# Shifting the SBUF addresses of the matmul operands in a fused two-block transformer kernel

## What is computed

```
first_block:  x += g1 * mixer(modulate(rms_norm(x)));  x += g2 * swiglu(modulate(rms_norm(x)), w_ffn_in, w_ffn_out)
              mixer = s5 state space (layer 0), short convolution (layer 1); then rms_norm(x, final_g)
second_block: x = layer_norm(ALPHA*x + mixer(x));      x = layer_norm(ALPHA*x + squared_relu_mlp(x))
              mixer = dilated window attention (layer 0), HGRN2 linear attention (layer 1)
```

## Time and profile before

| | us |
|---|---|
| median of 3 runs | 2748.53 |
| the profiled execution, its own time | 2751.34 |
| its span, first to last instruction | 2749.6 |
| PE busy | 2660.2 (97%) |
| DVE busy | 1490.2 (54%) |
| ACT busy | 1049.2 (38%) |
| POOL busy | 109.3 (4%) |

### The profile page before, as it was taken

How to read it: one execution, slowest core, us unless ns; L and a number is a source line. 1 busy time by engine, 2 the same in 40 slices (tenths; PEclk the granted TensorE clock), 3 DMA queues, 4 the chain that set the end, 5 groups by cost and what they waited for, 6 DMA issues and landing times.

```text
span 2749.6 us, 38093 instructions
## 1 busy us (share of the span) xinstructions
PE 2660.2 (97%) x15914; PEld 2227.6 (81%) x15914; DVE 1490.2 (54%) x2230; ACT 1049.2 (38%) x1496; POOL 109.3 (4%) x118
## 2 busy tenths in 40 slices
PE   5999999999999999999999999999999999999998
PEld 2668888888898888888888887888889888888887
DVE  8958555556463333465555555744336675833335
ACT  3534312223233222255555554522223555522223
POOL 4800000000000000000000000000000000000000
PEclk7999999999999999999999999999999999999998
DMA  5054544432323222322222222132221121233220
GB/s 237 2 202 174 214 184 184 184 123 69 100 93 123 92 92 92 103 75 70 74 77 78 74 70 93 56 106 98 92 106 58 62 97 57 77 107 106 93 93 31
DMA packets 46102, 282.89 MB, mean 103 GB/s; under 512 B 6113, under 2 KB 8545, under 8 KB 19954
## 3 DMA queue, kind: packets, MB, share of 16 engines
q1 hardware_dynamic: 40002, 238.02, 25.1%
q0 software_dynamic: 5936, 42.51, 4.2%
HBM read 278.41 MB, written 2.10 MB: 102 GB/s over the span
## 4 chain that ended last, share of the span: by engine, by line
PE 79%; DVE 14%; ACT 4%; issue 2%; DMA 1%; POOL 0%; DVEq 0%; ACTq 0%
PE PS L646 17%; PE PS L647 17%; PE PS L648 17%; PE PS L781 4%; PE PS L783 4%; PE PS L782 4%; PE PS L870 1%; DVE Wl L1547 1%; PE PS L810 1%; PE PS L811 1%; PE PS L812 1%; DMA adab<-adaw 1%; PE PS L739 1%; PE PS L737 1%; PE PS L738 1%
## 5 line engine op out<-in xcount | busy, mean ns | idle before, releaser
L646 PE MATMUL PS<-Hl,Wh 128*128 128x512 f32 x1256 | 490.5, 391 | 7.2 <-DVE Wl L1547 7.2
L647 PE MATMUL PS<-Hh,Wl 128*128 128x512 f32 x1256 | 489.8, 390 | 0.0
L648 PE MATMUL PS<-Hh,Wh 128*128 128x512 f32 x1256 | 489.8, 390 | 0.0
L1133 ACT CAST Wh<-raw 128x2048 fp32r<-128x2048 f32 (+2 forms) x164 | 294.6, 1842 | 416.3 <-PE PS L648 395.8
L1547 DVE TENSOR_TENSOR Wl<-raw,Wh 128x2048 fp32r<-128x2048 f32 (+2 forms) x164 | 356.0, 2210 | 74.9 <-ACT Wh L1133 74.7
L646 PE MATMUL PS<-Gl,Wh 128*128 128x512 f32 x880 | 347.8, 395 | 0.0
L648 PE MATMUL PS<-Gh,Wh 128*128 128x512 f32 x880 | 347.6, 395 | 0.0
L647 PE MATMUL PS<-Gh,Wl 128*128 128x512 f32 x880 | 347.6, 395 | 0.0
L646 PEld LDWEIGHTS PS<-Hl,Wh 128*128 128x128 f32 x1256 | 236.6, 188 | 57.1 <-DVE Wl L1547 7.9
L648 PEld LDWEIGHTS PS<-Hh,Wh 128*128 128x128 f32 x1256 | 236.5, 188 | 49.6
L647 PEld LDWEIGHTS PS<-Hh,Wl 128*128 128x128 f32 x1256 | 236.5, 188 | 49.1
(11 more groups left out here) (419 smaller groups left out, 4802.5 us busy)
## 6 DMA issues: line engine op xcount, KB each, us to landing
raw<-wstream SPq DMA_DIRECT2D x152, 1024.0 KB, 6.3
raw<-wstream SPq DMA_DIRECT2D x64, 768.0 KB, 4.5
adab<-adaw POOLq DMA_DIRECT2D x40, 1024.0 KB, 5.8
raw<-wstream SPq DMA_DIRECT2D x20, 512.0 KB, 4.0
raw<-adap SPq DMA_DIRECT2D x4, 1024.0 KB, 10.0
ada_land<-adap SPq DMA_DIRECT2D x4, 1024.0 KB, 18.9
X<-xT SPq DMA_DIRECT2D x1, 2048.0 KB, 8.3
XU<-xU SPq DMA_DIRECT2D x1, 2048.0 KB, 14.4
```

The costliest lines, as they stand in the source:

```text
L646: mm(o, Wh[:, s, c0:c0 + P], xl[:, k, :], start=k == 0, stop=False)
L647: mm(o, Wl[:, s, c0:c0 + P], xh[:, k, :], start=False, stop=False)
L648: last = mm(o, Wh[:, s, c0:c0 + P], xh[:, k, :], start=False, stop=k == kt - 1)
L1133: nc.scalar.copy(w_high(p, h, widths[h]), raw[:, h, 0:widths[h]]).then_inc(split_h, 1)
```

## The change

```diff
         X = sb("X", [P, KT, T])
+        cst = sb("cst", [P, 3 * P + 4])
+        ident, ones_d, ones_h = cst[:, 0:P], cst[:, P:2 * P], cst[:, 2 * P:3 * P]
+        NRM = sb("NRM", [P, 5, KT])
+        sq = sb("sq", [P, 2, T])
+        Rn = sb("Rn", [P, T])
         land = ExitStack()
-        ada_land = [sb("ada_land" + str(i), [P, HALF], c=land) for i in range(4)]
+        ada_land = [sb("ada_land" + str(i), [P, HALF], c=land) for i in range(2)]
+        sb("gap_land", [P, 4, KT], c=land)
+        ada_land += [sb("ada_land" + str(i), [P, HALF], c=land) for i in range(2, 4)]
         land.close()
         Gh = sb("Gh", [P, KT, T], F32R)
+        LB = sb("LB", [P, 4, KT])
         Gl = sb("Gl", [P, KT, T], F32R)
         raw = sb("raw", [P, 2, HALF])
-        cst = sb("cst", [P, 3 * P + 4])
-        ident, ones_d, ones_h = cst[:, 0:P], cst[:, P:2 * P], cst[:, 2 * P:3 * P]
-        MODS = sb("MODS", [P, 96])
-        NRM = sb("NRM", [P, 5, KT])
-        AM = sb("AM", [P, 4, KT])
-        LNP = sb("LNP", [P, 8, KT])
-        CW = sb("CW", [P, 3, KT])
-        HG = sb("HG", [P, KT])
-        LB = sb("LB", [P, 4, KT])
         S5D = sb("S5D", [P, KT])
-        sq = sb("sq", [P, 2, T])
-        Rn = sb("Rn", [P, T])
...
         pad = sb("pad", [P, 384], c=s5)
+        sb("gap5", [P, 8], c=s5)
         AB_U = sb("AB_U", [P, 8, 16], c=s5)
...
         JS = sb("JS", [1, 8, P], c=s5)
+        sb("gap5b", [P, 736], c=s5)
         prm = sb("prm", [P, 24, 32], c=s5)
...
         Hh = sb("Hh", [P, KT, T], F32R)
+        sb("gap", [P, 8])
         Hl = sb("Hl", [P, KT, T], F32R)
...
+        HG = sb("HG", [P, KT])
+        MODS = sb("MODS", [P, 96])
+        LNP = sb("LNP", [P, 8, KT])
+        AM = sb("AM", [P, 4, KT])
+        CW = sb("CW", [P, 3, KT])
         tmp = sb("tmp", [P, 4, T])
```

## The result

The changed kernel takes 2772.73 us in the median of four runs (2772.43 to 2774.22), the kernel before 2749.7 us in four (2744.04 to 2751.68): a ratio of 1.0089 with a 95% interval of 1.0074 to 1.0104. It is slower by 23 us. The forecast was 2735 us, faster; the measured time lies inside the stated range (2655 to 2780), on the other side of the forecast, 6 us from the time of the slower rival.

What follows compares the result with a forecast made beforehand. TensorE, busy 97%, was taken to bound the kernel by matmul count and price. Terms -18.7 + 4.2 + 0.9 = -13.6 us against the profiled 2751.3 us gave 2737.7, in terms of the median 2735 us; range 2655 to 2780 us.

Steps and rivals of the forecast that it cites:

- slower rival: Distance 0 alone is good: G stays at 233.4 ns, Hh joins it; 18.8 us more, 2767 us, chance 0.24.
- What bounds the kernel: TensorE, busy 97% of the span: the number of matmuls and the price of one, read from start to start.
- Step 3, H: Matmuls streaming Hl and Hh, 5328 of 512 columns and 2400 of 256: no change taken for either buffer.
- the G state: Spacing of matmuls streaming Gl or Gh before the change: 233.4 ns with 512 columns, 116.7 with 256; a bound for H.
- Step 1, G with 512 columns: 2832 matmuls streaming Gl and Gh go from 233.4 to 226.8 ns: 18.7 us less.
- Step 2, G with 256 columns: 1440 matmuls streaming G take over H's state, 2.9 ns more each: 4.2 us more.
- H's state: Spacing of matmuls streaming Hl or Hh before the change: 226.8 ns with 512 columns, 119.5 with 256.
- Step 4, what else moves: Shifted VectorE and ScalarE buffers: 0.9 us lost to a wait in the first G products, 0 for the state space stage.
- Deeper gain: New distances free streams of part or all of their surcharge: all 174 us, half taken, 2662 us, chance 0.21.
- The rule of the ports: TensorE's moving and weight read ports are independent and never wait, so no placement matters and the sum is 0.

Runs made afterwards that it cites:

- hh_on_weights: The changed kernel with the 32 byte gap in front of Hh instead of behind it, so Hh, Hl and weights begin on multiples of 2048: 2740.89 us, ratio to before 0.998.
- m1_table: Separate kernel of only float32r matmul streams, 48 per choice of weight and moving offsets, other engines idle; 512 columns: 226.7 ns at 864/864, 233.3 at 864/128.
- m2_512: Separate stream kernel, 512 columns, all 512 combinations of Wl, low and high moving offsets in 32 byte steps: lowest 226.7 ns, median 232.2, worst 236.6.
- m4_leads: Separate stream kernel: five placements, each entered 16 times after one matmul of 16 to 256 columns; two values at 192 and 32 with 256 columns, distance 0 one.
- all_at_64: The changed kernel with Gh, Gl, Hh and Hl all 64 bytes above a multiple of 256, weights on a multiple of 2048: 2748.53 us, ratio 0.9997.
- m5_next_or_own: Separate stream kernel with weights taken in turn from two areas, then plain float32 streams at eight distances; no alternating stream at 226.7 ns, plain 215.8 and 429.2 ns.

## Why the prediction was wrong

- *What bounds the kernel* was right: TensorE's spacing made the whole difference. Reading starts instead of shown lengths was what made it visible.
- *Step 3, H.* This step failed. It took no change for Hh, "as its absolute place within 64 bytes stays what it was". The absolute place means nothing; the distance had gone from 0 to 32 below, and that cost 30 us on H with 512 columns (1229.3 to 1259.3 us), all of which `hh_on_weights` gave back (1226.4 us) by moving Hh alone. Nor did Hl keep its value: the three matmuls of the body slow down together, to 231, 234 and 235 ns, a mean of 233.3. With 256 columns the step missed a gain of 3.4 us (H -1.1, streamed weights -2.3). The text had the right bound there ("the G state") and chose the other end.
- *Step 1, G with 512 columns.* The sign was right, the size not: 230.4 ns instead of 226.8, and 6.8 us instead of 18.7. Distances of 64 and 192 below are better than 32 beyond and worse than 0.
- *Step 2, G with 256 columns:* +1.4 us for +4.2. The 2.9 ns were read in one place; elsewhere in the kernel before the same G streams hold 117.8 ns and not 116.7. In the layout where G really takes H's state it is +4.9 (+6.2 in the second trace), so that price was about right and the state was not reached.
- *Step 4, what else moves*, was right: casts and subtractions unchanged, 0.5 us more idle before L651. After Hh is put back, what remains is 7.2 us of gain, of which G's sums give 6.9; so no noticeable share of the loss lies in the small buffers or the state space stage. The 0.9 us for a wait in the first G products weren't tested by themselves.
- *The slower rival* named the cause, the place and nearly the size: 18.8 us worked out, 23 measured. That it came so near is in part luck, for its errors nearly cancel. It left out Hl (H with 512 columns took 30.0 us more, not 23.4), it left G unchanged (-6.8 us), and its gain with 256 columns was 4.6 us for 2.0 measured. Its own test, Hl at 227 beside Hh at 233, would have failed.
- *The choice between them.* The forecast and this rival explained the rows equally well, and the forecast needed two guesses about distances that no row had. With evidence for one good distance and one bad one, the plain reading was that leaving the good one costs, for the 3552 matmuls that left it; the 2832 of G that might gain moved to two distances without a row. The chances of 0.34 and 0.24 had it the other way about.
- *Deeper gain:* none of the 512 combinations is below 226.7 ns with 512 columns. The plain float32 row was taken as a sign that the surcharge could vanish. It could not be carried over: those streams run at half the rate and show no address at all.
- *The rule of the ports:* the Trainium skill (SBUF — State Buffer, "Who interferes with whom") lets TensorE's two read ports work without waiting for each other. What the prediction drew from it, that no placement matters, the measurement refutes for float32r: 226.7 to 240.0 ns for one and the same instruction, by addresses alone, with every other engine idle. Whether it is the two ports that wait for each other isn't shown.
- The Trainium skill (TensorE: Matmul & The Clock Gate, "Back-to-back issue gap") gives 2.5 ns over the columns' time, and calls this the gap of a single matmul, not that of a stream of load and matmul pairs. The plain float32 streams agree (429.2 ns for 2 x 213.3); no float32r stream with a new weight load for each matmul does (13.4 ns at best with 512 columns, 6.6 with 256). The about 131 ns that this section of the Trainium skill gives for such pairs with 512 columns were seen in no run here either.

## What to carry over

When TensorE is at 97%, read the spacing of matmul starts for each pair of operand buffers before anything else, and compare it with columns over clock; here the difference between two buffers that run through the same line was a matter of addresses. For float32r streams of 512 columns with a fresh weight load each, place moving buffers and weights at the same offset modulo 256 bytes: here that alone gave 0.4%, and 32 bytes of misplacement of one buffer cost 1.1%. With 256 columns distance 0 is not the best (120.0 ns, other distances down to 113.3). Small tables are enough to shift big buffers, and a table of spacings over all offsets fits into one run of a kernel that does nothing else.

## What the hardware showed

- Where all operands of a float32r stream of 512 columns share one distance between moving operand and weights, the spacing depends on it modulo 256 bytes (`m1_table`): 226.7 ns at 0, 228.9 at 64, 232 to 234 elsewhere in steps of 32, 240.0 at 20 bytes, the worst seen. The absolute place doesn't matter. Where the offsets differ (`m2_512`), no single distance tells it, and one such placement is as good as 0.
- With 256 columns the order is another (113.3 to 124.4 ns, 120.0 at distance 0); with 384 and 128 columns the three distances tried (0, 32, 64) gave one value each, 173.3 and 111.7 ns.
- At some placements a stream has two settled spacings: 113.3 and 117.8 ns with 256 columns at distance 192, depending on the width of the one matmul ahead of it (`m4_leads`); 228.9 and 233.3 ns in `all_at_64`, kept over several products in a row, the higher one where the clock was still at its lower level when the stream began. Distance 0 showed one. Why was not settled.
- Plain float32 streams, each matmul with its weight load, cost 215.8 ns (256 columns) and 429.2 ns (512) at all eight distances (`m5_next_or_own`).
